# Input and memory laid out transposed by the host, inner layer norms transposed before gain and bias, in a one-core transformer layer

## The reference

```python
x = layer_norm(a * x + 0.5 * swiglu(x, ffn1_gate, ffn1_up, ffn1_down), ln1_g, ln1_b)   # norm 1
x = layer_norm(a * x + hybrid_mixer(x, w_in, ...), ln2_g, ln2_b)                       # norm 2
x = layer_norm(a * x + memory_cross_attention(x, mem, ...), ln3_g, ln3_b)              # norm 3
x = layer_norm(a * x + 0.5 * swiglu(x, ffn2_gate, ffn2_up, ffn2_down), ln4_g, ln4_b)
```

## Time and profile before

| | |
|---|---|
| median of 3 runs | 2330.62 us (2328.92 to 2330.88) |
| span of the profiled execution, first to last instruction | 2327.1 us |
| median less that span | 3.5 us |
| PE busy, of the span | 97% |
| VectorE, ScalarE, GpSimd busy | 52%, 44%, 2% |
| mean granted TensorE clock | 0.990 |

### The profile page before, as it was taken

One profiled execution on the slowest core, in us unless ns is written; L12 is line 12 of the kernel. 1 busy time (PEld: TensorE's weight loads), 2 busy tenths in 40 slices (PEclk: granted clock), 3 DMA queues, 4 the chain that ended last, 5 costly groups with the idle time before them and its releaser, 6 DMA issues.

```text
span 2327.1 us, 26221 instructions
## 1 busy us (share of the span) xinstructions
PE 2263.6 (97%) x10486; PEld 1883.4 (81%) x10486; DVE 1218.7 (52%) x1269; ACT 1019.0 (44%) x1088; POOL 48.1 (2%) x34
## 2 busy tenths in 40 slices
PE   8999999999999999999999999997999999999996
PEld 6888888888888788888888877786888888898885
DVE  4544544455446545467556664456544454454445
ACT  4444444344334455555454443334444444443332
POOL 0000000000001100000000020001000000000001
PEclk9999999999999999999999999998999999999998
DMA  7555555465555455557346544453555555575552
GB/s 254 188 191 184 195 181 197 163 239 190 193 193 212 156 184 175 177 168 272 120 134 218 180 163 145 152 192 126 189 189 185 193 182 196 169 241 193 192 192 80
DMA packets 217084, 427.17 MB, mean 184 GB/s; under 512 B 6832, under 2 KB 23472, under 8 KB 216368
## 3 DMA queue, kind: packets, MB, share of 16 engines
q1 hardware_dynamic: 214336, 413.16, 52.5%
q10 hardware_dynamic: 2672, 12.93, 1.5%
HBM read 423.97 MB, written 2.10 MB: 183 GB/s over the span
## 4 chain that ended last, share of the span: by engine, by line
PE 93%; DVE 4%; ACT 1%; DMA 1%; issue 1%; POOL 0%; ACTq 0%; DVEq 0%; POOLq 0%
PE ps_A L489 45%; PE ps_B L489 42%; PE ps_T L505 2%; DVE wlo L921 2%; DVE x_tok L1359 1%; PE ps_T L864 1%; PE ps_T L851 1%; ACT whi L911 0%; PE ps_B L767 0%; PE ps_T L793 0%; DVE x_tok L1364 0%; DMA raw<-in_mem_wk_dram 0%; DMA stage<-in_mem_dram 0%; PE ps_T L638 0%; PE ps_T L802 0%
## 5 line engine op out<-in xcount | busy, mean ns | idle before, releaser
L921 DVE TENSOR_TENSOR wlo<-raw,whi 128x1024 fp32r<-128x1024 f32 (+1 forms) x792 | 965.9, 1222 | 1048.4 <-ACT whi L911 1047.4
L911 ACT ACTIVATE whi<-raw 128x1024 fp32r<-128x1024 f32 (+1 forms) x792 | 827.6, 1047 | 1196.9 <-PE ps_A L489 638.5
L489 PE MATMUL ps_A<-whi,xT_hi 128*128 128x512 f32 (+1 forms) x704 | 275.3, 391 | 8.4 <-DVE wlo L921 4.5
L489 PE MATMUL ps_A<-whi,xT_lo 128*128 128x512 f32 (+1 forms) x704 | 272.4, 387 | 0.0
L489 PE MATMUL ps_A<-wlo,xT_hi 128*128 128x512 f32 (+1 forms) x704 | 272.2, 387 | 0.0
L489 PE MATMUL ps_B<-whi,xT_hi 128*128 128x512 f32 (+1 forms) x704 | 270.3, 384 | 0.0
L489 PE MATMUL ps_B<-wlo,xT_hi 128*128 128x512 f32 (+1 forms) x704 | 270.3, 384 | 0.0
L489 PE MATMUL ps_B<-whi,xT_lo 128*128 128x512 f32 (+1 forms) x704 | 270.3, 384 | 0.0
L489 PEld LDWEIGHTS ps_A<-whi,xT_hi 128*128 128x128 f32 x704 | 133.3, 189 | 35.5 <-issue 8.8
L489 PEld LDWEIGHTS ps_A<-whi,xT_lo 128*128 128x128 f32 x704 | 133.1, 189 | 25.5
L489 PEld LDWEIGHTS ps_A<-wlo,xT_hi 128*128 128x128 f32 x704 | 133.4, 189 | 24.4
(11 more groups left out here) (279 smaller groups left out, 2864.2 us busy)
## 6 DMA issues: line engine op xcount, KB each, us to landing
raw<-in_ffn_gate_dram SPq DMA_DIRECT2D x80, 1024.0 KB, 4.9
raw<-in_ffn_up_dram SPq DMA_DIRECT2D x80, 1024.0 KB, 4.8
raw<-in_ffn_down_dram SPq DMA_DIRECT2D x80, 1024.0 KB, 5.1
raw<-in_w_in_dram SPq DMA_DIRECT2D x44, 1024.0 KB, 4.9
raw<-in_mem_wk_dram SPq DMA_DIRECT2D x16, 1024.0 KB, 5.1
raw<-in_mem_wv_dram SPq DMA_DIRECT2D x16, 1024.0 KB, 5.1
raw<-in_w_out_dram SPq DMA_DIRECT2D x16, 1024.0 KB, 5.1
raw<-in_mem_wq_dram SPq DMA_DIRECT2D x16, 1024.0 KB, 5.1
```

The lines of the kernel that those rows point to most:

```text
L489: mm = pe.matmul(ps[pair][:, t * W:t * W + n], lhs[a][:, kt, t * P:(t + 1) * P], w[:, slot, q * n:(q + 1) * n], start=first and q == 0 and ...
L911: act.activation(whi[:, c % AHEAD, 0:n], raw[:, slot, o:o + n], ACT.Copy).then_inc(hi_made, 1)
L921: dve.tensor_tensor(wlo[:, c % AHEAD, 0:n], raw[:, slot, o:o + n], whi[:, c % AHEAD, 0:n].bitcast(F32), ALU.subtract).then_inc(lo_made, 1)
```

## The change

The host passes `xT` and `memT`, as [128, 16, 256] with a kt's 256 tokens side by side, and `ln_col`, g and b of three norms with their columns down the partitions.

Head: no transposes. `xT` is loaded to `xraw` (four kts in two loads by ScalarE, three loads of four kts by SP), split by `x_split` on ScalarE and VectorE. Chunk 0's weights come in two halves, rounded and used half by half. GpSimd clears a tile with which PE does NWARM matmuls first. `x` token-major is loaded later, in SP's queue before the last gate block of FFN 1, for `norm_add`.

`mem`: the quarters of `memT` are split straight from `stage`, with no transposes.

Inner norms: PE turns a group as soon as ScalarE's `norm_piece` is done, four groups at chunks 4 to 7 of C_K0 and C_V3. `norm_split` on ScalarE applies g and b to the transposed group, four ACTIVATEs of 128x256 from PSUM to `xf`, and VectorE makes both parts from `xf`. The token-major copy gets its g and b from VectorE alone, in `norm_full`, later: chunks 1 to 4 of C_WIN and C_WQ, 4 to 7 of FFN 2. The last norm keeps its form (`norm_last`, and GpSimd's four adds).

The diff's core, its indentation cut; C_V3 and C_WQ are edited as C_K0 and C_WIN are.

```diff
+xraw = sb("xraw", [P, KD, T], F32, o_H + 64 * KB)
+xf = [sb(f"xf{i}", [P, 4, T], F32, o_H + (80 + 4 * i) * KB) for i in range(2)]
...
+            for k in range(2):
+                sp.dma_start(raw[:, 0, k * W:(k + 1) * W], g[k * P:(k + 1) * P, 0:W]).then_inc(w_first[k], 16)
+            sp.dma_start(raw[:, 0, CHUNK:].rearrange("p (k w) -> p k w", w=W),
+                         cols_of(g, 2, 4, 0, W)).then_inc(landed[0], 16)
+            for k in range(1, 4):
+                sp.dma_start(xraw[:, 4 * k:4 * k + 4, :], d["xT"][:, 4 * k:4 * k + 4, :]).then_inc(x_in[k], 16)
                 piece(k, k, cols_of(g, 4 * k, 4 * k + 4, 0, W), W, False)
...
+        if f == 1:
+            sp.dma_start(x_tok[:, :, :], d["x"].rearrange("(t p) n -> p t n", p=P)).then_inc(xt_in, 16)
...
-        pe.wait_ge(lo_made, c + 1)
+        if not (type(c) is int and c == 0):
+            pe.wait_ge(lo_made, c + 1)
         for q, kt in enumerate(kts):
+            if type(c) is int and c == 0:
+                pe.wait_ge(w_first_lo if q == 0 else lo_made, 1)
...
-                if b == 0 and f == 1 and m in S_MEM:
-                    g = S_MEM.index(m)
-                    pe.wait_ge(mem_in[g], 16)
-                    turn_group(("mem", g), lambda t, i: stage[g % 2][:, t, i * P:(i + 1) * P])
...
-        w_normed(pe, 4 * i + g + 1)
+        pe.wait_ge(norm_hat, (4 * i + g + 1) * TT)
...
+    def x_wait(k):
+        if k < 0:
+            pe.wait_ge(freed[B], 1)
+            pe.wait_ge(freed[T0], 1)
+            for i in range(NWARM):
+                pe.matmul(ps[T0][:, 0:T], warm[:, 0:P], warm[:, T:W], start=True, stop=True,
+                          skip_group_check=True)
+        elif k < 2 or k % 2 == 0:
+            pe.wait_ge(x_lo, k + 1 if k < 2 else k // 2 + 2)
+        elif k == 7:
+            pe.wait_ge(ident_in, 16)
+    half_ffn(1, C_FFN1, xT0, x_wait)
...
+    pe.wait_ge(mem_lo, 4)
     for k in range(8):
-        if k >= 6:
-            norm_group(0, k - 6)
+        if k >= 4:
+            norm_group(0, k - 4)
...
-                if k in (1, 3):
-                    norm_group(0, 2 + k // 2)
                 if k == 5:
                     kt_group(0)
                 if k % 2 == 0:
-                    w_over(pe, ("x1", k // 2))
+                    pe.wait_ge(xn_lo, k // 2 + 1)
...
+    def x3_group(k):
+        if k < 0:
+            norm_group(2, 0)
+        elif k % 2 == 0:
+            pe.wait_ge(xn_lo, 8 + k // 2 + 1)
+        elif k < 7:
+            norm_group(2, k // 2 + 1)
+    half_ffn(2, C_FFN2, xT3, x3_group)
...
+    def norm_split(i, g):
+        name = (f"x{i + 1}", g)
+        p, _ = U.at[name]
+        if (i, g) == (0, 0):
+            act.wait_ge(lncol_in, 16)
+        w_ready(act, name)
+        if 4 * i + g >= 2:
+            act.wait_ge(xn_lo, 4 * i + g - 1)
+        for k in range(4):
+            kt = 4 * g + k
+            e = act.activation(xf[g % 2][:, k, :], ps[p][:, k * T:(k + 1) * T], ACT.Identity,
+                               bias=lncol[:, i, 1, kt:kt + 1], scale=lncol[:, i, 0, kt:kt + 1])
+        e.then_inc(freed[p], 1)
...
+            act.wait_ge(mem_in[g], 16)
+            act.activation(memT[0][:, 4 * g:4 * g + 4, :], mem_kt(g), ACT.Copy).then_inc(mem_hi, 1)
+        if b == 0 and m - 2 in S_MEM[0:2]:
+            g = S_MEM.index(m - 2)
+            act.wait_ge(mem_lo, g + 1)
+            load_mem(g + 2)
...
+    for k in range(2):
+        act.dma_start(xraw[:, 2 * k:2 * k + 2, :], d["xT"][:, 2 * k:2 * k + 2, :]).then_inc(x_first[k], 16)
     act.dma_start(ident, d["const"][:, 0:P]).then_inc(ident_in, 16)
-    for c in range(AHEAD):
-        if c % 2 == 0:
-            group_hi(("x", c // 2), xT0, 2 * c)
+    act.dma_start(lncol[:, :, :, :], d["ln_col"]).then_inc(lncol_in, 16)
+    def x_split(a, b):
+        act.activation(xT0[0][:, a:b, :], xraw[:, a:b, :], ACT.Copy).then_inc(x_hi, 1)
+    act.wait_ge(x_first[0], 16)
+    x_split(0, 2)
+    for k in range(2):
+        act.wait_ge(w_first[k], 16)
+        act.activation(whi[:, 0, k * W:(k + 1) * W], raw[:, 0, k * W:(k + 1) * W], ACT.Copy).then_inc(
+            (w_first_hi, hi_made)[k], 1)
+    act.wait_ge(x_first[1], 16)
+    x_split(2, 4)
+    act.wait_ge(landed[0], 16)
+    for c in range(1, AHEAD):
         make_hi(act, c)
+        act.wait_ge(x_in[c], 16)
+        x_split(4 * c, 4 * c + 4)
...
+        if k >= 5:
+            norm_split(0, k - 5)
...
+                    norm_split(0, 3)
+                if k == 6:
+                    act.wait_ge(x_full, 1)
...
+            if f == 2 and k in (3, 5):
+                norm_split(2, k // 2 + 1, xT)
+            if f == 2 and k >= 4:
+                norm_full(2, k - 4, gb3)
             make_lo(dve, c0 + k + AHEAD)
...
+    def norm_split(i, g, dst):
+        dve.wait_ge(freed[U.at[(f"x{i + 1}", g)][0]], U.at[(f"x{i + 1}", g)][1] + 1)
+        kts = slice(4 * g, 4 * g + 4)
+        dve.tensor_copy(dst[0][:, kts, :], xf[g % 2][:, :, :]).then_inc(xn_hi, 1)
+        dve.wait_ge(xn_hi, 4 * i + g + 1)
+        dve.tensor_tensor(dst[1][:, kts, :], xf[g % 2][:, :, :], dst[0][:, kts, :].bitcast(F32),
+                          ALU.subtract).then_inc(xn_lo, 1)
+    def norm_full(i, g, gb):
         if g == 0:
             dve.wait_ge(gb_in[i], 16)
-        cols, done = slice(g * W, (g + 1) * W), (4 * i + g) * TT
+        cols = slice(g * W, (g + 1) * W)
+        for j, op in enumerate((ALU.mult, ALU.add)):
+            for t in range(TT):
+                e = dve.tensor_tensor(x_tok[:, t, cols], x_tok[:, t, cols], gb[:, j, cols], op)
+                if j == 0:
+                    did(e)
+            if j == 0:
+                see()
+            elif g == 3:
+                e.then_inc(x_full, 1)
...
+            dve.wait_ge(mem_hi, g + 1)
+            kts = slice(4 * g, 4 * g + 4)
+            dve.tensor_tensor(memT[1][:, kts, :], mem_kt(g), memT[0][:, kts, :].bitcast(F32),
+                              ALU.subtract).then_inc(mem_lo, 1)
...
+    def x_split(n, a, b):
+        dve.wait_ge(x_hi, n)
+        dve.tensor_tensor(xT0[1][:, a:b, :], xraw[:, a:b, :], xT0[0][:, a:b, :].bitcast(F32),
+                          ALU.subtract).then_inc(x_lo, 1)
+    x_split(1, 0, 2)
+    for k in range(2):
+        dve.wait_ge((w_first_hi, hi_made)[k], 1)
+        dve.tensor_tensor(wlo[:, 0, k * W:(k + 1) * W], raw[:, 0, k * W:(k + 1) * W],
+                          whi[:, 0, k * W:(k + 1) * W].bitcast(F32), ALU.subtract).then_inc(
+            (w_first_lo, lo_made)[k], 1)
+    x_split(2, 2, 4)
+    for c in range(1, AHEAD):
         make_lo(dve, c)
+        x_split(c + 2, 4 * c, 4 * c + 4)
...
-        if 1 <= k <= 4:
-            norm_piece(0, k - 1, gb1)
-        if k >= 6:
-            group_lo(("x1", k - 6), x1T, 4 * (k - 6))
+        if k >= 5:
+            norm_split(0, k - 5, x1T)
         make_lo(dve, C_K0 + k + AHEAD)
...
+            if n == 0 and k == 0:
+                norm_split(0, 3, x1T)
+            if n == 0 and 1 <= k <= 4:
+                norm_full(0, k - 1, gb1)
...
+    dve.wait_ge(x_full, 1)
...
+        if s == 39:
+            dve.wait_ge(x_full, 2)
```

More of the change, by code:

```diff
@@ L180, in acc @@
         u.take(("acc", c), pair)
-    for g in range(4):
-        u.take(("x", g), g, True)
     for f, c0 in ((1, C_FFN1), (2, C_FFN2)):
@@ L186, in turns @@
             for g in range(4):
-                u.take(("x3", g), T0 + g % 2, True)
+                u.take(("x3", g), T0 + g % 2)
         acc(c0, A)
@@ L195, in turns @@
             u.take(("d", f, b), (A, B)[b % 2])
-            if f == 1 and b == 0:
-                for g in range(4):
-                    u.take(("mem", g), (T1, T0)[g % 2], True)
         if f == 2:
@@ L202, in turns @@
         for g in range(4):
-            u.take(("x1", g), T0 + g % 2, True)
+            u.take(("x1", g), T0 + g % 2)
         u.take(("kt", 0), T0)
@@ L237, in turns @@
         for g in range(4):
-            u.take(("x2", g), T0 + g % 2, True)
+            u.take(("x2", g), T0 + g % 2)
         for s in range(64):
@@ L374, in hybrid_layer @@
         x_in = [sem(f"x_in{g}") for g in range(4)]
+        x_first = [sem(f"x_first{i}") for i in range(2)]
+        w_first = [sem(f"w_first{i}") for i in range(2)]
+        w_first_hi, w_first_lo = sem("w_first_hi"), sem("w_first_lo")
+        x_hi, x_lo, mem_hi, mem_lo = sem("x_hi"), sem("x_lo"), sem("mem_hi"), sem("mem_lo")
+        xt_in, lncol_in = sem("xt_in"), sem("lncol_in")
         mem_in = [sem(f"mem_in{g}") for g in range(4)]
@@ L1208, in _ @@
                     norm_piece(1, k - 1)
-                if k >= 6:
-                    group_hi(("x2", k - 6), x2T, 4 * (k - 6))
+                if k >= 5:
+                    norm_split(1, k - 5)
                 make_hi(act, C_V3 + k + AHEAD)
@@ L1223, in _ @@
             for s in range(64):
-                if s in (1, 3):
-                    group_hi(("x2", 2 + s // 2), x2T, 8 + 4 * (s // 2))
+                if s == 0:
```

(45 more changed lines are left out.)

86 lines of the change are left out of this document (26 added, 60 removed).

## The result

The changed kernel took 2306.93 us (median of 4 runs, 2303.93 to 2309.53) against 2329.77 for the kernel before (median of 4, 2328.70 to 2330.88): a ratio of 0.9903, 95% interval 0.9889 to 0.9917, 22.8 us less. The prediction was 2304.5, range 2297 to 2314, so the time is 2.4 us above it and inside the range.

The account below looks back on a forecast made before the run. TensorE, busy 97% of the span, was taken as the bound. Head 7.5, `mem` 6.2, norm 1 5.9, norm 2 7.4, norm 3 -0.95 sum to 26.1; 2330.6 - 26.1 = 2304.5 us, range 2297 to 2314.

Parts of the forecast that it names:

- Head, 7.5: Start of the kernel to the ninth chunk: no transposes, first product at 6.4, 7.5 us gained.
- Chunk 0 slow: 6.4 to 11.5: Head: the first chunk runs at the lower clock despite the warm-up matmuls, from 6.4 to 11.5 us.
- the data wait: Head: chunk 4 waits for the last quarter of `x` and starts at 21.2 in place of 19.6.
- mem, 6.2: `mem` stage: transposes and PE's waits go, the landing wait moves to ScalarE with slack 5; 6.2 us gained.
- Norm 1, 5.9: C_K0's start to the gates: no slow chunk, waits of 1.1 for T0 and 1.2 for gate weights; 5.9 us gained.
- Norm 2, 7.4: C_V3's start to WQ's ninth chunk: norm 1's schedule without gates, 1.1 for T0, 0.5 for `wlo` 16; 7.4 us gained.
- Norm 3, 0.95 lost: To the eighth chunk's end: first chunk 1.65 earlier, then three waits of 1.35, 1.5 and 1.5; 0.95 us lost.
- Elsewhere 0: Outside head, `mem` and inner norms: no gap of PE touched, no new PE instruction, so 0 us.
- The longer chain (1): In each norm, six operations from transposes to product; splits 1.5 longer than counted would give 2313.5 us; chance 0.09.
- VectorE as the bound (2): Behind the norms: operations at 1.19 make `norm_full` 4.8, gain about 2; slower above 5.0, 2338 at 5.6; chance 0.03.
- Early transposes that hide nothing (3): Norms: first product after waits as long for T0 or `wlo`; only head and `mem`, 13.7, remain: 2317 us; chance 0.04.
- All short (4): Chunk 4 without a wait, splits at 1.5, no wait for gates: gain 33, 2297.5 us; chance 0.06.

Follow-up runs that it names:

- e3: Changed kernel with norm 3's groups transposed earlier (two before chunk 0, then before chunks 1 and 3), splits moved to match: 2298.61 us.
- e8: Changed kernel with 16 filler matmuls in the wait for `hc` and the 32 narrow score matmuls in two halves: 2305.55 us.
- e10: Changed kernel with norm 3 early, norms 1 and 2 spread, last quarter of `x` later, clock edits, and fillers in norm 3's waits: 2291.16 us.
- e4: Only the head and `mem` parts of the change, the three inner norms as in the kernel before: 2315.75 us.
- e1: The changed kernel run again without an edit, for a second trace: 2307.04 us.

## Why the prediction was right, and where it was not

- **The whole.** 2306.93 against 2304.5. The gain was 22.8 against 26.1 counted, so the sum is 3.3 too high; the base, 0.85 too high as well, hid part of that, which is luck. Head, `mem` and norms 1 and 2 are right by mechanism and size. Two terms are off, norm 3 in size and "elsewhere" altogether.
- **Head, 7.5: right (7.8).** First product at 6.99 against 6.4 said, mostly since `xT` landed at 4.9 and not at 4.35; chunk 4 at 20.69 against 21.2. The last quarter landed at 17.06 where the row of before gave 17.9. The step "Chunk 0 slow: 6.4 to 11.5" was wrong; its reason was norm 3, where PE did 2 us of transposes and then waited 3. In the head it did 4.6 us of matmuls and waited 0.9. It cost nothing because the next step, the data wait, was right. The Trainium skill's 358 GB/s ("DMA: Bandwidth & Descriptors", Specifications) would have put the landing 1 us later; the trace moved 389 to 403 GB/s between 4 and 17 us, so it doesn't agree with that figure, and the quarter landed 0.8 earlier than I had it.
- **mem, 6.2: right (6.0).** No wait of PE there, and none for `raw` around the 2 MB load of `x_tok`.
- **Norm 1, 5.9: right (6.0)**, with both waits (1.0 for 1.1, 0.8 for 1.2). **Norm 2, 7.4: right (7.3)**; the 0.5 for `wlo` 16 wasn't seen. The granted clock was 1.00 through both, from 740 to 772 and from 1310 to 1359.
- **The prices.** A split's ACTIVATEs have 0.56 us each and 0.45 from start to start, 1.90 to 1.92 for four (1.85 taken). The formula of the Trainium skill ("VectorE: DVE Perf Modes", TRN2 errata) gives an estimated 1.4, which this trace doesn't bear out. A `norm_full` took 2.61 (2.6 taken). In the window of norm 1:

```profile
L1414 DVE TENSOR_TENSOR x_tok<-x_tok,gb 128x512 f32<-128x512 f32 x16 | 10.3, 686 | 0.1
L993 ACT ACTIVATE xf<-ps_T,lncol 128x256 f32<-128x256 f32 x16 | 7.7, 560 | 0.0
```

- **Norm 3, 0.95 lost: right in mechanism, mis-sized (2.3).** First product 7.60 behind the pieces (7.5 said), waits of 1.26, 1.41 and 1.38 (1.35, 1.5, 1.5 said). The failed term is "5.1 + 7 x 2.72": the slow chunk took 5.4, and each of the three chunks behind a wait 3.03, together 1.2 of the 1.4 that are missing (the waits themselves were 0.3 shorter than said, and the pieces came 0.3 later, counted from WQ's ninth chunk). Both sizes stood in the prediction's rows: the slow chunk of norm 3 itself with 5.46, and a chunk behind a wait with 2.99. e3 got the waits and the longer chunks back, and a part of the slow chunk.
- **"Elsewhere 0": wrong**, by 1.8 to 5.5 in a trace. The step that failed is "Elsewhere PE has no gap that the change touches, and it gets no new instruction there". It looked for instructions, but the stretch behind the compressed products holds a gap and a light piece of work. Behind them the granted clock was 1.00 in both traces of the kernel before, and fell behind one or both of them in six of eight traces with the change or a part of it; with both places filled or split (e8 to e10) it fell in none of three. What shifts between executions stays open.
- **The base.** 3.5 us "around the span" were 1.8, and the three runs shown had a median 0.9 above that of four.
- **Rivals.** The longer chain (1) took back only what was counted. VectorE as the bound (2) had the wrong price for its operations (686 ns, not 1190) but was right that it binds: at 5.2 for a `norm_full` the kernel is slower than before, 2338.9, where "above 5.0" was said. It still asked too little, since it gives 2338 only at 5.6. On a straight line between the two measured points (2.6 and 5.2) the kernel would be level with the one before near 4.5, an estimate; nothing between them was run. Early transposes that hide nothing (3): e4 against e1 shows 8.7 in the norms. All short (4): no part of it.
